# A mixture-of-experts decoder trunk on one Trainium2 core: where two engines leave the loop of an expert, how two norms are divided, and how two weight loads are cut

## The chip, the core and the metric

The kernel runs on one core of one Trainium2 chip. TensorE (PE in the profile) multiplies, VectorE (DVE), ScalarE (ACT) and GpSimd (POOL) work on elements, SyncE (SP) issues nearly all transfers, and 16 DMA engines move them. Each engine runs its own program; they meet at semaphores. The metric is the device time of the whole program in microseconds (us), median of the runs.

## What is computed

Two layers over 256 tokens of 1024 features, all in float32. Each layer: a mixer, cross-attention into 256 memory tokens, and a mixture of 32 experts of which each token takes 2. After each of the three, `x = LayerNorm(alpha * x + f(x))`. Cut to what matters here:

```
for layer in range(2):
    mix = even_mixer(x) if layer == 0 else (B * conv3(C * h)) @ w_out     # B, C, h = split(x @ od_w_in, 3)
    x = layer_norm(alpha * x + mix, ...)
    x = layer_norm(alpha * x + cross_attention(x, mem_k, mem_v), ...)
    x = layer_norm(alpha * x + moe(x), ...)        # moe: sum over the 2 experts of a token of
                                                   # gate * ((silu(x @ w1) * (x @ w3)) @ w2)
```

Each expert has three matrices of 2 MB (w1 and w3: 1024 x 512, w2: 512 x 1024). All 32 experts of both layers are read once: 192 matrices, about 400 MB of the 477 MB that the program moves.

## The kernel before

Tokens lie in two tiles of 128 (`TT = 2`). Twelve places in SBUF hold expert matrices: six of a ring, three named ones (SPARE, GAINS, HELD) and three slots (6, 7, 8) that serve the mixer and the attention in other stages. Four experts at a time have their three matrices in them (`SETS = 4`), and eight turns (`TURNS`) go over the 32 experts. GAINS also holds, in its first half (columns 0 to 2047), the gain and bias rows of the current norm (`gb`), and slot 8 holds the queries (first half) and the attention's output (second half).

**SP** issues the loads strictly in the order of its program, and each may wait for its place to come free. The first twelve are `first_load` (L435 on); the load of expert 2's w1 into GAINS stands last, behind the wait for both tiles of x (L457, L458). Then `next_expert` (L464) loads expert e + 4 when expert e has given its places back: w1 and w3 once the hidden product is done (`hid_done`), w2 once the result is (`y_done`). For the very last expert w3 and w2 are loaded in two transfers, 3072 columns (`MOST`) and then 1024, so that PE can begin before the rest has landed.

**PE** works by units of up to 32 tokens of one expert. An expert with more tokens has more units (m of them). A unit on PE is: `scatter` of the unit before (L1070), `turn` (L1051), `gather` of the next unit (L1028), `results` with w2 (L1062), and then `hidden` of the next unit with w1 and w3 (L1044). Before the hidden product of the last expert `keep_warm` issues `WARM = 18` products with zeros (L515).

**DVE** and **ACT** follow unit by unit. DVE: `build` the selection of the next unit (L1575), `silu_in`, `glu_out`, `turn` (L1589, L1594, L1599), `take` (L1585), `weight` (L1580). ACT: tanh (L1855), and the copies L1859 and L1861. Their loop over the units of an expert is a nest: 4 times `Fori` with an `If`, and in each 2 times an `If`, whatever m is. PE's loop leaves by a branch when m is reached.

**The norm behind the experts** starts from four PSUM banks that hold both tiles, q = 0 to 3 being four quarters of the features. DVE takes statistics (L1229), aggregates (L1168), POOL computes `rstd` (L1940, L1941), DVE the shift (L1237). ACT writes the normalized tile 0 (four operations, L1282) and half of tile 1, DVE the other half of tile 1 (L1252). PE transposes both tiles (L536), ACT (L1295) and DVE (L1174) write them into `xT`, and the mixer of layer 1 begins with `od_c0` by tile (L574) and goes on by weight (L566). In the last norm ACT writes both tiles, and DVE multiplies by the gain and adds the bias in four pairs of 512 columns (L1266, L1267); SP sends out four pieces in order (L496).

Of the kernel before, what the change touches and what calls it, by code (L numbers as in the profile page):

```python
# [58 lines left out]
WARM = 18  # L59
# [31 lines left out]
def program(nc, T, out):  # L91
    ctx = ExitStack()
    with ctx:
# [110 lines left out]
        rest_in = {m_: sem(f"rest_in_{('w1', 'w3', 'w2')[m_]}") for m_ in (1, 2)}  # L204
# [46 lines left out]
        dve_plain = sem("dve_plain")  # L251
        out_ready = sem("out_ready")
# [88 lines left out]
        def _(sp):  # L341
# [68 lines left out]
            for L in range(DEPTH):  # L410
# [24 lines left out]
                def first_load(e, m_):  # L435

                    s = slots[e][m_]
                    wait_free(s)
                    if e == SETS - 1 and m_:
                        sp.sem_inc(rest_in[m_], 16)  # L440
                    sp.dma_start(slot_ap(s), expert_weights(PARTS[m_], L, e)).then_inc(loaded[s], 16)

                for m_ in range(3):
                    first_load(0, m_)
                first_load(1, 0)
# [5 lines left out]
                first_load(2, 1)  # L451
                if L == 0:
                    sp.wait_ge(mem_kept, 16)
# [10 lines left out]
                def next_expert(e, j, last=False):  # L464

                    m, first = load_units(sp, L, e)
                    for m_ in range(3):
                        s = slots[j][m_]
                        sp.wait_ge(used_up[m_], first + m)
                        if m_ and last and j == SETS - 1:  # L470
                            src = expert_weights(PARTS[m_], L, e + SETS)
                            sp.dma_start(slot_ap(s)[:, 0:MOST], src[:, 0:MOST]).then_inc(loaded[s], 16)
                            sp.dma_start(slot_ap(s)[:, MOST:4096], src[:, MOST:4096]).then_inc(rest_in[m_], 16)
                            continue
                        if m_ and j == SETS - 1:
# [16 lines left out]
            for t in range(TT):  # L492
                for done, h in enumerate((1, 0)):
                    hh = slice(512 * h, 512 * (h + 1))
                    sp.wait_ge(out_ready, 2 * t + done + 1)
# [5 lines left out]
        def _(pe):  # L501
# [15 lines left out]
            def normal(i, t):  # L517

                if i % 3 == 2:
                    pe.wait_ge(act_plain[t], sum((Q, Q // 2)[t] for j in range(2, i + 1, 3)))  # L520
                    if t == 1:
                        pe.wait_ge(dve_plain, Q // 2 * (i // 3 + 1))
# [3 lines left out]
            def turned(key, src, t, warm=0, halves=(0, 1)):  # L526

                for h in halves:
                    ps = claim(pe, (key, t, h))
# [335 lines left out]
            for L in range(DEPTH):  # L865
                if L == 1:

                    for h in range(2):
                        wait_loaded(pe, f"od_c{h}")
                        pss = [claim(pe, ("odc", 4 * h + c)) for c in range(4)]  # L870
                        for c in range(4):
                            if h == 0 and c == 0:
                                for t in range(TT):
# [1113 lines left out]
```

## Time and profile before

| | us |
|---|---|
| median of 3 runs (lowest, highest) | 1385.27 (1383.77, 1385.79) |
| the profiled execution | 1383.4 |
| its span from first to last instruction | 1381.6 |
| PE busy | 1145.1 (83%) |
| DVE, ACT, POOL busy | 393.6, 168.8, 28.5 |
| mean granted TensorE clock | 0.929 |
| moved over the span | 477.40 MB, mean 346 GB/s |

The span is cut into 40 slices of 34.5 us in the page's second part. Two stretches stand out, about 310 to 712 us and 965 to 1365 us: the expert stages, in which DMA is 99% busy at 426 to 430 GB/s. Between and before them PE is at 9 tenths and the transfers pause at times.

### The profile page before, as it was taken

What the parts mean: (1) busy time and instruction counts of PE and PEld (TensorE: products, weight loads), DVE (VectorE), ACT (ScalarE), POOL (GpSimd) and SP (SyncE); (2) the same over time, 40 slices, a digit from 0 to 9 for tenths busy, and PEclk for the clock granted to TensorE, in tenths of its full rate; (3) what the DMA queues carried; (4) which work ended last, traced back from release to release, by engine and by line L of the source; (5) the groups of instructions that cost most, each with busy time, mean ns of one, the idle gap of its engine ahead of it and who ended that gap; (6) DMA issues with size and microseconds to landing.
All of it is one profiled execution on the core that took longest, in us unless ns stands there. A gap on an engine that the chain in (4) does not pass through costs nothing.

```text
span 1381.6 us, 33102 instructions
## 1 busy us (share of the span) xinstructions
PE 1145.1 (83%) x11896; PEld 731.1 (53%) x11897; DVE 393.6 (28%) x1030; ACT 168.8 (12%) x470; POOL 28.5 (2%) x83
## 2 busy tenths in 40 slices
PE   8999999987997677668699999999897767757756
PEld 7885558554553344335358867655454433434333
DVE  1972632342231221112132133253222111211213
ACT  1212502110110000001020001111110000000001
POOL 3000000000000000000000000000000000000000
PEclk9999999998998988889899999999999887888888
DMA  9756058499999999999996657465999999999996
GB/s 347 250 183 244 9 189 342 186 352 426 429 427 430 427 429 428 428 429 428 429 406 251 243 197 319 182 236 207 426 427 430 427 430 427 428 429 428 428 428 258
DMA packets 68378, 477.40 MB, mean 346 GB/s; under 512 B 8364, under 2 KB 13772, under 8 KB 43500
## 3 DMA queue, kind: packets, MB, share of 16 engines
q1 hardware_dynamic: 66284, 470.27, 83.0%
q0 software_dynamic: 2048, 6.47, 1.4%
q8 instruction: 34, 0.56, 0.2%
q14 instruction: 12, 0.10, 0.0%
HBM read 473.58 MB, written 3.15 MB: 345 GB/s over the span
## 4 chain that ended last, share of the span: by engine, by line
PE 56%; DMA 31%; SPq 5%; issue 4%; DVE 2%; another core or an unknown queue 1%; ACT 1%; ACTq 1%; POOL 0%; DVEq 0%
DMA slot<-in_moe_w_dram 20%; PE bank L566 12%; PE bank L1044 12%; DMA ring<-in_moe_w_dram 10%; PE bank L589 8%; SPq L477 5%; PE bank L1062 4%; PE bank L1070 3%; PE bank L1028 2%; PE bank L574 2%; PE bank L775 2%; PE bank L929 1%; PE bank L947 1%; PE bank L623 1%; PE bank L515 1%
## 5 line engine op out<-in xcount | busy, mean ns | idle before, releaser
L1044 PE MATMUL bank<-ring,xT 128*32 128x256 f32 x1920 | 177.7, 452 | 43.3 <-DMA ring<-in_moe_w_dram 43.3
L1044 PE MATMUL bank<-slot,xT 128*32 128x256 f32 x1120 | 163.7, 457 | 2.2 <-issue 2.2
L566 PE MATMUL bank<-xT,ring 128*128 128x256 f32 x656 | 143.3, 379 | 0.7 <-PE bank L566 0.7
L1044 PE MATMUL bank<-held,xT 128*32 128x256 f32 x608 | 89.1, 458 | 56.6 <-DMA slot<-in_moe_w_dram 46.4
L1044 PEld LDWEIGHTS bank<-ring,xT 128*32 128x32 f32 x1920 | 91.3, 129 | 84.1 <-issue 64.5
L566 PEld LDWEIGHTS bank<-xT,ring 128*128 128x128 f32 x656 | 124.1, 190 | 17.7 <-issue 1.1
L1589 DVE SCALAR_TENSOR_TENSOR xT<-xT,bank 64x256 f32<-64x256 f32 x73 | 30.3, 415 | 348.7 <-ACT xT L1855 348.6
L1044 PE MATMUL bank<-spare,xT 128*32 128x256 f32 x512 | 78.7, 475 | 45.6 <-DMA ring<-in_moe_w_dram 43.2
L589 PE MATMUL bank<-ring,slot 128*128 128x512 f32 x256 | 111.4, 593 | 0.8 <-PE bank L566 0.8
L1062 PE MATMUL bank<-ring,xT 128*32 128x256 f32 x1824 | 109.6, 381 | 1.9 <-DVE xT L1599 1.5
L1044 PE MATMUL bank<-gains,xT 128*32 128x256 f32 x512 | 74.5, 455 | 36.1 <-DMA slot<-in_moe_w_dram 36.1
L1070 PE MATMUL bank<-xT 32*128 32x256 f32 x1200 | 86.6, 400 | 21.2 <-issue 20.0
L1044 PEld LDWEIGHTS bank<-held,xT 128*32 128x32 f32 x608 | 48.2, 131 | 91.9 <-issue 78.7
L1575 DVE TENSOR_TENSOR xT<-iota,place 128x64 f32 (+1 forms) x73 | 16.4, 225 | 276.2 <-issue 273.6
L1855 ACT ACTIVATE xT<-bank 64x256 f32<-64x256 f32 x73 | 27.6, 377 | 516.3 <-PE bank L1044 494.3
L1070 PEld LDWEIGHTS bank<-xT 32*128 32x128 f32 x1200 | 55.1, 184 | 56.7 <-issue 53.5
L1044 PEld LDWEIGHTS bank<-spare,xT 128*32 128x32 f32 x512 | 42.0, 135 | 78.2 <-issue 68.4
L1062 PEld LDWEIGHTS bank<-ring,xT 128*32 128x32 f32 x1824 | 60.5, 110 | 42.4 <-issue 8.5
L1028 PE MATMUL bank<-x,xT 128*32 128x256 f32 x1200 | 81.2, 388 | 0.0
L589 PEld LDWEIGHTS bank<-ring,slot 128*128 128x128 f32 x256 | 48.2, 190 | 59.1 <-issue 59.0
L1044 PEld LDWEIGHTS bank<-slot,xT 128*32 128x32 f32 x1120 | 75.0, 131 | 3.2 <-issue 2.7
L1044 PEld LDWEIGHTS bank<-gains,xT 128*32 128x32 f32 x512 | 39.0, 130 | 66.3 <-issue 54.0
(290 smaller groups left out, 1110.1 us busy)
## 6 DMA issues: line engine op xcount, KB each, us to landing
ring<-in_moe_w_dram SPq DMA_DIRECT2D x94, 2048.0 KB, 46.4
slot<-in_moe_w_dram SPq DMA_DIRECT2D x46, 2048.0 KB, 48.3
held<-in_moe_w_dram SPq DMA_DIRECT2D x16, 2048.0 KB, 39.2
spare<-in_moe_w_dram SPq DMA_DIRECT2D x16, 2048.0 KB, 46.9
gains<-in_moe_w_dram SPq DMA_DIRECT2D x16, 2048.0 KB, 47.0
ring<-in_od_w_in_dram SPq DMA_DIRECT2D x6, 2048.0 KB, 21.2
ring<-in_xa_wq_dram SPq DMA_DIRECT2D x4, 2048.0 KB, 11.5
ring<-in_xa_wo_dram SPq DMA_DIRECT2D x4, 2048.0 KB, 12.5
```

The costliest lines, as they stand in the source:

```text
L477: sp.dma_start(slot_ap(s), expert_weights(PARTS[m_], L, e + SETS)).then_inc(loaded[s], 16)
L566: ins = mm(ps, w[:, k, c0:c0 + P], rhs[:, k, :], start=(k == 4), stop=(k == 3))
L574: ins = mm(ps[:, t * P:(t + 1) * P], w[:, k, c0:c0 + P], xT[:, k, t * P:(t + 1) * P], start=(k == 4), stop=(k == 3))
L589: ins = mm(ps[:, :], oT[:, k, t * P:(t + 1) * P], ws[h][:, k, :], start=(k == 0), stop=(k == KC - 1))
L775: ins = mm(ps[:, :], memT[:, k, t * P:(t + 1) * P], w[:, k, :], start=(k == 0), stop=(k == KC - 1))
L1028: ins = mm(bX[qs[q], 0:w], d[:, t, :], x[:, t, q * w:(q + 1) * w], start=(t == 0), stop=(t == TT - 1))
L1044: ins = mm(b1[qs[2 * m + h], 0:S], xg[:, k, :], ws[m][:, k, h, :, :], start=(k == 0), stop=(k == KC - 1))
L1062: ins = mm(bY[qs[q], 0:n], hidT[:, c, :], w[:, c, q * n:(q + 1) * n], start=(c == 0), stop=(c == 3))
L1070: ins = mm(acc[q][:, t * n:(t + 1) * n], cb[qs[q], t * P:(t + 1) * P], yy[qs[q], :], start=False, stop=final and t == TT - 1, skip_group_c ...
L1575: tt(disp, iota[:, at_].unsqueeze(1).to_broadcast([P, TT, CAP]), column(place, e).to_broadcast([P, TT, CAP]), ALU.is_equal).then_inc(fam.d ...
L1589: stt(out=glu, in0=th, scalar=1.0, in1=banks[5][0:P // 2, 0:S], op0=ALU.add, op1=ALU.mult).then_inc(fam.glu_done, 1)
L1855: act(th, banks[5][0:P // 2, 0:S], ACT.Tanh, scale=0.5).then_inc(fam.tanh_done, 1)
```

## The change

1. **Loops.** On DVE and ACT the nest over an expert's units becomes one `Fori` over up to 8 rounds with one branch out of it when the last unit is done, as PE has it.
2. **Early halves.** Half of the w1 of expert 2 (GAINS, columns 2048 to 4095) is loaded right behind expert 0's, once `wo_mix` is done, and half of the w2 of expert 3 (slot 8, columns 0 to 2047) once the attention is done with the queries. The other halves stay where the whole loads were. Both layers.
3. **The last expert.** w1 and w3 are both cut at 3072 columns, and the transfers go w1 and w3 up to 3072, then w1 and w3 from there, then w2 as before. `WARM` is 12 instead of 18.
4. **Norm of layer 0's experts.** Both tiles are divided alike: ACT writes quarters 2 and 3, DVE quarters 0 and 1. Tile 0 is written, transposed and put into xT before tile 1. The 4 warm products between the two tiles go.
5. **Mixer of layer 1.** PE does column group 0 of `od_c0` for tile 0, then transposes tile 1, then group 1 for tile 0, then groups 0 and 1 for tile 1, then 2 and 3 by weight. The banks of PSUM are given out accordingly.
6. **Last norm.** DVE computes (psum - mean) * gain for both tiles from PSUM (eight operations of 256 columns). For tile 0 ACT multiplies by rstd and POOL adds the bias; for tile 1 DVE does both in one operation per 512 columns.

```diff
-WARM = 18
+WARM = 12
@@ SP: first loads
+                early_load(2, 0, (weights_used, order.index(f"wo_mix{L}b") + 1), gains_early)
                 first_load(1, 0)
...
                 first_load(2, 1)
+                early_load(3, 2, (xa_done, L + 1), queries_early)
@@ SP: next_expert
+                    if last and j == SETS - 1:
+                        for parts in ((0, 1), (2,)):
+                            sp.wait_ge(used_up[parts[0]], first + m)
+                            for m_ in parts:
+                                s = slots[j][m_]
+                                src = expert_weights(PARTS[m_], L, e + SETS)
+                                sp.dma_start(slot_ap(s)[:, 0:MOST], src[:, 0:MOST]).then_inc(loaded[s], 16)
+                            for m_ in parts:
+                                s = slots[j][m_]
+                                src = expert_weights(PARTS[m_], L, e + SETS)
+                                sp.dma_start(slot_ap(s)[:, MOST:4096], src[:, MOST:4096]).then_inc(rest_in[m_], 16)
+                        return
@@ PE: mixer of layer 1
+                        if h == 0:
+                            pss = [claim(pe, ("odc", c), bank=6 + c) for c in range(2)]
+                            by_tile(2, "od_c0", 0, pss[0], 0)
+                            turned(("n", 2), x, 1, at=(4, 5))
+                            by_tile(2, "od_c0", P, pss[1], 0)
+                            for c in range(2):
+                                by_tile(2, "od_c0", c * P, pss[c], 1)
+                            pss += [claim(pe, ("odc", c), bank=c - 2) for c in range(2, 4)]
+                            rotation[0] = 4
@@ DVE: norm behind the experts
             stats(0, range(Q))
             moments(0)
             stats(1, MOE_ORDER[:2])
-            shifts(0)
+            if i < LAST_NORM:
+                shifts(0)
+                plain_part(0)
             stats(1, MOE_ORDER[2:])
             moments(1)
             if i < LAST_NORM:
+                to_xT(st, v, i, 0)
                 shifts(1)
+                plain_part(1)
...
             else:
...
+                        nc.vector.scalar_tensor_tensor(out=x[:, t, cols_], in0=ps[:, t * n:(t + 1) * n], scalar=mv[:, t, 0:1],
+                                                       in1=gb[:, 0, cols_], op0=ALU.subtract, op1=ALU.mult).then_inc(centred[t], 1)
...
+                    nc.vector.scalar_tensor_tensor(out=x[:, 1, hh], in0=x[:, 1, hh], scalar=rstd[:, 1, :], in1=gb[:, 1, hh],
+                                                   op0=ALU.mult, op1=ALU.add).then_inc(out_ready[1], 1)
@@ DVE: the loop of an expert
-                    with v.Fori(0, ROUNDS // 2) as ra:
-                        with v.If(m > ra * 2):
-                            with v.Fori(0, 2) as rb:
-                                with v.If(m > ra * 2 + rb):
+                    with v.Fori(0, ROUNDS) as r:
...
+                        v.br_lt(v.to_reg(m - r), 2, on_true=f"moe{L}_rows_next", on_false=f"moe{L}_rows_again")
@@ ACT: the last norm (the loop is changed as DVE's)
+                        act(x[:, 0, hh], x[:, 0, hh], ACT.Identity, scale=rstd[:, 0, :]).then_inc(scaled, 1)
@@ POOL: the last norm
+                    nc.gpsimd.tensor_tensor(x[:, t, hh], x[:, t, hh], gb[:, 1, hh], ALU.add).then_inc(out_ready[t], 1)
```

## Rows read from the trace of the kernel before

**Rows 1.** Windows: stretch, its us, busy by engine, granted clock, DMA share, GB/s

```profile
306.00:308.00 2.00, 2.00 (x45) 1.09 (x39) 0.00 (x0) 0.37 (x1) 0.00 (x0) 1.00 0.66 172
...
960.00:962.00 2.00, 2.00 (x44) 1.18 (x38) 0.00 (x0) 0.37 (x1) 0.00 (x0) 1.00 0.00 0
```

**Rows 2.** Timeline of SP: start, us, line, transfers issued, early in both expert stages

```profile
306.07 8.46 SPq L477 DMA_DIRECT2D ring<-in_moe_w_dram  x4
...
945.00 23.90 SPq L477 DMA_DIRECT2D ring<-in_moe_w_dram  x4
```

**Rows 3.** DMA issues between 306 and 307 us: size, us from issue to landing

```profile
ring<-in_moe_w_dram SPq DMA_DIRECT2D x1, 2048.0 KB, 8.4
```

**Rows 4.** Chain that ended last, in time: start, us, what, at both stages' begin

```profile
295.87 4.32 issue
...
951.32 1.93 PE bank L1062 x32
...
959.15 1.73 PE bank L1062 x32
```

**Rows 5.** Timelines of ACT and DVE in layer 1: [idle before it, until whom]

```profile
949.26 0.38 ACT L1855 ACTIVATE xT<-bank 64x256 f32<-64x256 f32 x1 [3.88 <-PE bank L1044]
...
952.62 0.23 DVE L1575 TENSOR_TENSOR xT<-iota,place 128x64 f32 x1 [0.62 <-DVE xT L1580]
...
972.11 0.23 DVE L1575 TENSOR_TENSOR xT<-iota,place 128x64 f32 x1 [4.52 <-issue]
```

**Rows 6.** Timeline, last expert of layer 1

```profile
1355.78 4.06 PE L515 MATMUL bank<-zero 128*128 128x512 bf16 x18
...
1364.78 0.19 POOL L1950 TENSOR_TENSOR vare<-vare,half 128x1 f32<-128x1 f32 x1 [447.64 <-DMA slot<-in_moe_w_dram]
...
1366.08 1.91 PE L1062 MATMUL bank<-slot,xT 128*32 128x256 f32 x32
```

**Rows 7.** Timeline of SP: the cut loads of w3, layer 1

```profile
1312.01 4.24 SPq L472 DMA_DIRECT2D ring<-in_moe_w_dram  x1
1316.29 4.24 SPq L473 DMA_DIRECT2D ring<-in_moe_w_dram  x1
```

**Rows 8.** DMA issues between 1300 and 1330 us: the same two, us to landing

```profile
ring<-in_moe_w_dram SPq DMA_DIRECT2D x1, 1536.0 KB, 47.7
...
ring<-in_moe_w_dram SPq DMA_DIRECT2D x1, 512.0 KB, 44.7
```

**Rows 9.** Timeline, norm behind layer 0's experts and begin of layer 1's mixer

```profile
720.76 1.93 ACT L1282 ACTIVATE x<-bank,shift,rstd 128x256 f32<-128x256 f32 x4 [4.14 <-DVE shift L1237]
721.43 0.26 DVE L1168 BATCH_NORM_AGGREGATE mv<-bn 128x2 f32<-128x24 f32 x1
...
722.74 1.17 PE L536 MATMUL bank<-ident,x 128*128 128x128 f32 x8 [1.80 <-ACT x L1282]
...
725.50 3.74 PE L574 MATMUL bank<-xT,ring 128*128 128x128 f32 x32
729.07 38.15 PE L566 MATMUL bank<-xT,ring 128*128 128x256 f32 x176
```

**Rows 10.** Timeline, last norm

```profile
1373.24 0.26 DVE L1168 BATCH_NORM_AGGREGATE mv<-bn 128x2 f32<-128x24 f32 x1
...
1373.89 0.92 POOL L1941 TENSOR_TENSOR rstd<-vare,half 128x1 f32<-128x1 f32 x1
...
1375.14 4.39 SPq L496 DMA_DIRECT2D out_dram<-x  x4
...
1378.47 0.69 DVE L1267 TENSOR_TENSOR x<-x,gains 128x512 f32<-128x512 f32 x1
```

**Rows 11.** Groups of POOL by form: count, busy us, mean ns, idle before

```profile
L1941 POOL TENSOR_TENSOR rstd<-vare,half 128x1 f32<-128x1 f32 x12 | 7.2, 599 | 1.0
...
L1890 POOL TENSOR_SCALAR residual<-ident 128x128 f32<-128x128 f32 x1 | 0.6, 564 | 0.1
```

**Rows 12.** Timeline of DVE in layer 0's convolution: 19 operations with a pointer scalar

```profile
52.63 7.60 DVE L1352 SCALAR_TENSOR_TENSOR slot<-slot,e 128x256 f32<-128x256 f32 x19
```

More of the change, by code:

```diff
@@ L250, in program @@
         act_plain = [sem(f"act_plain{t}") for t in range(TT)]
-        dve_plain = sem("dve_plain")
-        out_ready = sem("out_ready")
+        dve_plain = [sem(f"dve_plain{t}") for t in range(TT)]
+        out_ready = [sem(f"out_ready{t}") for t in range(TT)]
+        scaled = sem("scaled")
+        centred = [sem(f"centred{t}") for t in range(TT)]
         x_ready = [sem(f"x_ready{t}") for t in range(TT)]
@@ L469, in next_expert @@
                         sp.wait_ge(used_up[m_], first + m)
[L470 to L475, printed above, removed]
+                        if j == SETS - 1:
                             sp.sem_inc(rest_in[m_], 16)
@@ L1040, in hidden @@
                         if rest is not None and k * S * 2 == MOST:
+                            pe.wait_ge(rest_in[0], rest)
                             pe.wait_ge(rest_in[1], rest)
@@ L1113, in _ @@
                     start_sum(q, 1)
+                pe.wait_ge(gains_early, 16 * (L + 1))
+                pe.wait_ge(queries_early, 16 * (L + 1))
                 pe.wait_ge(units_ready, L + 1)
@@ L1275, in moe_norm_act @@
                 a.wait_ge(row_scale[t], L + 1)
-                for done, q in enumerate(MOE_ORDER):
-                    if t == 1 and i < LAST_NORM and q < 2:
-                        continue
+                for done, q in enumerate(MOE_ORDER[:2]):
                     ps = wait_filled(a, ("f", i, q))
@@ L1866, in _ @@
                     m, first = load_units(a, L, e)
-                    with a.Fori(0, ROUNDS // 2) as ra:
-                        with a.If(m > ra * 2):
-                            with a.Fori(0, 2) as rb:
-                                with a.If(m > ra * 2 + rb):
-                                    n = first + ra * 2 + rb + 1
-                                    first_half(fam, n)
-                                    second_half(fam, n, comb, y)
-                                a.nop()
+                    before = nc.cur_bb
+                    with a.Fori(0, ROUNDS) as r:
+                        n = first + r + 1
+                        first_half(fam, n)
+                        second_half(fam, n, comb, y)
+                        a.br_lt(a.to_reg(m - r), 2, on_true=f"moe{L}_tanh_next", on_false=f"moe{L}_tanh_again")
+                        nc.switch_bb(f"moe{L}_tanh_again")
                         a.nop()
-                moe_norm_act(a, 3 * L + 2)
+                    a.br(f"moe{L}_tanh_next")
+                    nc.switch_bb(f"moe{L}_tanh_next", parent=before)
                 if L + 1 < DEPTH:
-                    norm_act(a, 3 * L + 2)
+                    moe_norm_act(a, 3 * L + 2)
+                else:
+                    a.wait_ge(ln_rstd, 2 * LAST_NORM + 1)
+                    for done, h in enumerate((1, 0)):
+                        hh = slice(512 * h, 512 * (h + 1))
+                        a.wait_ge(centred[0], 2 * (done + 1))
+                        act(x[:, 0, hh], x[:, 0, hh], ACT.Identity, scale=rstd[:, 0, :]).then_inc(scaled, 1)
         @block.gpsimd
```

131 lines of the change are left out of this document (75 added, 56 removed).

## The prediction

> **What bounds the kernel now.** I read the page's second part first: it separates two stretches of saturated transfers from the stages ahead of them, in which PE is busy nearly all the time. So the program is a chain of five pieces: PE up to the first expert, a stream of weights, a compute tail with a norm and the second layer's mixer and attention, a second stream, and a last tail. A microsecond saved counts only if it lies in a piece's chain. Next I asked where each stream begins, since its length is fixed by bytes. In layer 0 the window 306 to 308 us has a DMA share of only 0.66 [rows 1]; SP issues at 306.07, when expert 0's result is done [rows 2], and that transfer lands after 8.4 us [rows 3]. One of 2 MB at 428 GB/s needs 4.9 us, so nothing was queued ahead of it: the stream starts there. In layer 1 the engines move nothing from 960 to 962 us [rows 1]. Four ring loads go out between 945.00 and 968.9 [rows 2]: the first is expert 0's w2, the next two expert 1's w1 and w3, at about 964.4, when its third hidden product ends. That is the start of the second stream. From there 81 matrices follow (96 less 12 preloaded and 3 sent earlier): 81 x 4.9 = 397 us, and 964.4 + 2 + 397 = 1363.4, which is where the saturated slices end. So both streams start when PE frees the places, and neither waits for the bytes before it.
>
> **Part 2, the early halves: nothing.** They take 1 MB each out of the queue ahead of the streams, 2.45 us apiece. But a stream that starts at a release finds the engines empty before the change too [rows 1, 3]; without the two halves they are idle somewhat longer. What they could cost: they go out in stages where later loads are for later experts, so a shift of 2.45 us meets no waiting PE, and their waits are the ones that the neighbouring load had anyway, so no queue is held. Bounds: 0 lost; gained at most what is idle in the windows 306 to 310 of layer 0, about 0.9 us (0.34 of 2 us [rows 1], and a little behind it), if PE's stall ahead of it shrank. I take 0.
>
> **Part 1, the loops.** DVE idles 4.52 us between the last work of one expert and the build for the next one when m is 1, and 0.62 us from one round to the next within an expert [rows 5]. How much of the 3.9 us between them is the nest's empty rounds, no row says; it is between 0 and 3.9, and I take the middle, 2, on DVE and ACT alike (each needs only 0.9 below). In the streams that is off the path, since PE itself waits for weights. In front of a stream it counts: at 949.26 ACT starts tanh 3.88 us after its last copy [rows 5], 0.9 us behind the end of the hidden product (it begins with the release at 945.00 and takes 3.4). PE has 2.5 us of scatter, turn and gather to cover it, and is late by the rest: a wait of 0.14 and a results product of 1.93 instead of 1.73 [rows 4], 0.34 us. Only one such change of expert (0 to 1) lies before the second stream's start, none before the first's. Gain 0.34 (0 to 0.5). Two places where loops end, ahead of both norms, have 4.14 us of slack on ACT [rows 9].
>
> The price of the branch out is not in this trace for DVE or ACT. PE has its form, and shows either nothing extra or a stall such as the 4.32 us "issue" at 295.87 [rows 4], the first time its loop runs. The Trainium skill (Runtime: NRT & Kernel Launch, Instruction fetch mechanics) says that a taken branch to code outside the two fetched pages waits for a fetch by DMA. By that rule the new exit could cost such a stall; whether it does depends on where the code falls. That is a rival below. I take 0 for it here.
>
> **Part 3, the last expert.** In both layers 18 warm products run from the end of results to the beginning of the last hidden product: 4.06 us from 1355.78 [rows 6], 0.2256 each, so six fewer are 1.35 us. They are on the path if the weights are there. Layer 1: the first part of w3 lands at 1312.01 + 47.7 = 1359.7, the rest at 1316.29 + 44.7 = 1361.0 [rows 7, 8]. With the old order, the hidden product would wait for 1359.7, and the six products would be worth 0.1 only. The new order takes 512 KB (1.2 us) of w1 out from in front: 1358.5, and warm ends at 1355.78 + 2.71 = 1358.5. The last two of eight steps come 2.6 us later, at 1361.1, against 1361.0 for the rest of w3, which is unchanged since the sum of the bytes is. Then w2: results start at 1366.08 - 1.35 = 1364.7, and POOL sees its first part at 1364.78 [rows 6]; the last quarter is wanted 1.4 us later and 512 KB behind. All four just fit. Gain 1.30, with 0.1 as the low end and 1.35 as the high one. In layer 0 the same things stand with more room (its warm ends 1.0 us later against its landings), so 1.35. PE is busy before and behind at a granted clock of 1.00, so fewer products lower nothing. Together 2.65.
>
> **Parts 4 and 5, the norm into the mixer.** Before: ACT's four operations end at 722.69 and PE transposes at 722.74; the tile products of column group 0 follow at 725.50 and 38.15 us for 11 groups by weight, 3.47 each, from 729.07 [rows 9]. So `od_c0` is done at 729.07 + 0.17 + 3 x 3.46 = 739.6 (0.17: the overlap of records). After: ACT writes two quarters by 720.76 + 1.93/2 = 721.7, DVE two of its own beside it, 0.40 each [rows 12]. Transposes 721.8 to 723.0. DVE's two push the last statistics and the aggregate from 721.43 to 722.2; rstd of tile 1 comes at most 1.6 us later (1373.24 to 1374.81 in the last norm [rows 10]); the four xT operations of tile 0, under 0.40 each, take 723.05 to 724.45, and only then come the shift and tile 1's quarters, 1.1 us, to 725.6. PE finishes group 0 of tile 0 at 724.75 and waits 0.9 us: transposes of tile 1 from 725.7 to 726.9, then three tile products of 3.58/2 = 1.79 to 732.2, then two by weight to 739.15. Gain 0.45. Ends: -0.5, if DVE's longer list puts tile 1 another 0.9 us back; +1.3, if PE's wait for tile 1 vanished. From here to the second stream PE is busy without a gap, so it counts in full.
>
> **Part 6, the last norm.** Everything in tile 1's statistics moves forward, because no shift is waited for: the aggregate at 1372.75 instead of 1373.24 [rows 10]. Then eight DVE operations of 256 columns from PSUM; one with a pointer scalar takes 7.60/19 = 0.40 [rows 12], so tile 0 is centred by 1373.8 (first half) and 1374.6, tile 1 by 1376.2, and its two final ones (0.69 each, as at 1378.47) end at 1377.6. ACT's multiplication of 512 columns is not in the trace; one of 256 takes 1.93/4 = 0.48 [rows 9], so it is between 0.48 and 0.96, and I take 0.8: 1374.6 and 1375.4. Then POOL, whose add of 128 x 512 is not in the trace either. Its only wide operation with arithmetic takes 564 ns for 128 columns [rows 11], its smallest some 190: 2.9 ns for a column, 1.6 us for 512. Two are 3.2 us, from 1374.6 to 1377.8. SP sends in order, tile 0 first: the third and fourth pieces, done at 1376.9 and 1377.6, queue behind POOL's, and the fourth goes at 1378.5, against about 1379.2 before (1375.14 + 4.39 less the issue itself) [rows 10]. Gain 0.65; POOL's L1941 took 0.92 at 1373.89, beside DVE's product of x and gains, against 0.599 in the mean [rows 10, 11], so I put 0.15 to that: 0.5. Ends: +1.5, if POOL keeps up and DVE is last; -1.2, if both adds are stretched as L1941 was (2.5 us each, the fourth piece at 1380.4).
>
> On this step the Trainium skill speaks against the change: GPSIMD Engine Reference (Engine selection; Key points) gives elementwise work to VectorE, says that GpSimd is about twice as slow for two inputs, and that it contends with a DVE instruction with two SBUF inputs. The row of L1941 agrees as to contention. An estimate from that page's 4497 ns for 2048 columns, by columns, is 1.1 us plus dispatch for one add; the sum would then be about 0.4 us better.
>
> **The sum.** 0 + 0.34 + 2.65 + 0.45 + 0.5 = 3.9 us off the profiled execution's 1383.4: 1379.5. That execution lies 1.9 below the median of the three, so I put the same difference there: 1385.27 - 3.9 = 1381.4.
>
> **The rivals.**
> *The streams are bound by their bytes.* Then the early halves would count: 2 MB in each layer, 4 x 2.45 = 9.8 us, and 1381.4 - 9.8 = 1371.6. Against it stand the idle windows just before both starts. For it, nothing in layer 1; in layer 0 the 0.9 us. Chance 0.04.
> *The landings take the warm products' place.* The four fits of part 3 have 0.1 us of room in layer 1. If a transfer more costs 0.5 us in each layer, or lands late, 2.65 becomes 1 to 1.5: 1382.8. Chance 0.13.
> *POOL becomes the end.* The low end of part 6: 1.7 worse, 1383.1. With the low end of parts 4 and 5 too, 1384. Chance 0.15.
> *Slower: code that has to be fetched.* PE has one stall of 4.32 us ahead of the first stream and none ahead of the second, in the same program text, so it hangs on where code and loads fall, and PE's code grows here. A stall of that size between 931 and 964 us, or from the new exits on DVE in that stretch, delays the second stream by 4.3, and in layer 0 gather and results ran 1.1 longer behind it at a lower clock: 5.4. It decides as soon as more than 3.9 of it lies before 964.4: 1381.4 + 5.4 = 1386.8, slower than before. Two such stalls: 1392. In the streams it costs nothing. Chance 0.12.
> *Better than the sum.* The layer 0 stall shrinks (0.9), POOL keeps up (1.0): 1379.5. Chance 0.11.
>
> **How the numbers follow.** The forecast has the remaining 0.45, with 1381.4. Its own bounds from the parts are about 1379.5 to 1383. Two in ten may be left out: the bytes rival and part of the slow one; so low 1378.3, high 1385.4. A measurement here tells apart about 0.2%, 2.8 us. Faster than 1382.5: most of the forecast (0.37 of 0.45), better (0.11), bytes (0.04), a third of the landings (0.05) and of POOL (0.05): 0.62. Slower than 1388.0: half of the slow rival, 0.07. Within: 0.31.
>
> **What would show it.** Two DMA windows of idle before the starts as now, and the transfer at about 306 us landing after 8.4 us again: the halves bring nothing. DVE's idle time before L1575 near 2.5 us instead of 4.5. L515 with 12 in 2.7 us in both layers, the last hidden product starting with no wait; a wait on DMA there is the second rival. PE idle about 0.9 us between the first tile products and the second transposes. The last out transfer released by POOL, with its adds at 1.6 us. An "issue" gap on PE or DVE of 2 us or more between the second stage's first unit and the stream's start is the slow rival; the prediction is wrong by as much as that gap.

## The result, and the profile after

The changed kernel takes 1376.03 us (median of 4 runs, 1375.57 to 1377.9) against 1384.66 for the kernel before beside it (1383.77 to 1385.79): ratio 0.9943, 95% interval 0.9930 to 0.9957. A second comparison, six runs on another occasion, gave 1377.52 against 1384.18: 0.9951 (0.9939 to 0.9963). So 6.7 to 8.6 us are gone by the medians, where 3.9 were forecast; both medians lie below the predicted range. One of the eleven executions of the kernel with GAINS's half alone took 4107.89 us and is not in its ratio.

The page of the changed kernel (span, busy time by engine, then the 40 slices):

```profile
span 1376.1 us, 30241 instructions
PE 1142.7 (83%) x11896; PEld 735.4 (53%) x11897; DVE 393.5 (29%) x1032; ACT 165.3 (12%) x462; POOL 30.5 (2%) x85
PEclk9999999998998898888999999999998888888888
DMA  9856059579999999999997657555999999999996
```

The shape is as before, with two saturated stretches. The difference has to be looked for piece by piece, so I cut the span at five events that both kernels have, and took a second profile of each kernel to see how far one profile can be trusted. The second profile of before is an execution of 1384.28 us. All values are us from one event to the next, each read off the start of a row in the timeline; the end is the page's span, which is given to 0.1 us:

| stretch | before | before, second | after | after, second | mean difference | forecast |
|---|---|---|---|---|---|---|
| start to first hidden product, layer 0 | 290.72 | 290.78 | 291.37 | 290.08 | 0.0 | 0 |
| to the warm products, layer 0 | 413.28 | 414.21 | 411.08 | 410.85 | -2.8 | 0 |
| to the first statistics (last expert) | 13.83 | 13.83 | 12.54 | 12.52 | -1.3 | -1.35 |
| to first hidden product, layer 1 (norm, mixer, attention) | 210.16 | 210.06 | 209.11 | 209.17 | -1.0 | -0.45 |
| to the warm products, layer 1 | 427.79 | 427.83 | 427.61 | 427.97 | 0.0 | -0.34 |
| to the first statistics (last expert) | 13.87 | 13.86 | 13.06 | 12.52 | -1.1 | -1.30 |
| to the end (last norm) | 11.95 | 11.94 | 11.33 | 11.29 | -0.6 | -0.5 |

The differences make 6.8 us. What the forecast lacked, 2.8 us net, is the size of the gain in the stretch for which it had nothing: the stream of layer 0 with what leads up to it. The misses of the other stretches are smaller and cancel. The zero of the first row is a mean of 291.37 and 290.08, so a single profile says little there.

What happens there, in the chain of waits of the changed kernel (start, us, what the chain ran through):

```profile
291.37 3.66 PE bank L1073 x64
295.04 1.49 PE bank L1026 x6
296.53 2.03 issue
298.55 1.15 PE bank L1099 x16
```

The "issue" gap behind expert 0 is 2.03 us; it was 4.32 [rows 4]. In this profile PE's clock, too, stayed up (not in every one with so short a gap, as shown further down). The windows (PE, PEld, DVE, ACT and POOL busy, then granted clock, DMA share, GB/s), first of after, then of before:

```profile
300.00:302.00 2.00, 2.00 (x41) 1.23 (x44) 0.76 (x2) 0.37 (x1) 0.00 (x0) 1.00 1.08 451
302.00:304.00 2.00, 2.00 (x40) 1.20 (x36) 0.23 (x1) 0.37 (x1) 0.00 (x0) 1.00 0.96 410
306.00:308.00 2.00, 1.71 (x26) 0.94 (x18) 1.04 (x4) 0.38 (x1) 0.00 (x0) 1.00 1.02 430
```

```profile
300.00:302.00 2.00, 1.81 (x22) 1.13 (x26) 1.48 (x5) 0.00 (x0) 0.00 (x0) 0.80 1.01 426
302.00:304.00 2.00, 2.00 (x20) 0.88 (x24) 0.10 (x1) 0.37 (x1) 0.00 (x0) 0.50 1.01 426
```

Before, the clock fell to 0.50 (1.2 GHz) behind the gap of 4.32 us and PE did 20 products in 2 us; after, it kept 1.00 (2.4 GHz) and did 40. And SP sends the transfer that opens the stream 11.5 us after the first hidden product, where it was 15.4: at 302.86 (SP's row, then the DMA answer for that issue: KB, us to landing).

```profile
302.86 8.48 SPq L500 DMA_DIRECT2D ring<-in_moe_w_dram  x4
ring<-in_moe_w_dram SPq DMA_DIRECT2D x1, 2048.0 KB, 10.7
```

It lands after 10.7 us, not 8.4 [rows 3]: now something is queued ahead of it, and the window 306 to 308 has a share of 1.02 where it had 0.66 [rows 1]. The stream of layer 0 no longer starts from empty engines.

How much that is worth can be read from the bytes. The rows below are the first 17 us behind the first hidden product and the rest up to the warm products, of before and then of after:

```profile
290.72:307.72 17.00, 12.68 (x172) 7.50 (x176) 3.88 (x14) 1.12 (x3) 0.00 (x0) 0.90 0.93 364
307.72:704.00 396.28, 306.71 (x4521) 175.29 (x4511) 84.26 (x245) 38.99 (x104) 0.00 (x0) 0.89 1.01 428
```

```profile
291.37:308.37 17.00, 14.68 (x222) 9.30 (x226) 5.50 (x19) 1.62 (x5) 0.00 (x0) 1.00 0.82 330
308.37:702.45 394.08, 302.97 (x4468) 176.66 (x4461) 82.31 (x240) 38.40 (x103) 0.00 (x0) 0.89 1.01 428
```

The rest runs at 428 GB/s in both, so its length is its bytes. In the first 17 us before moved 6.2 MB and after 5.6. But half of GAINS, 1.0 MB, had gone out long before in after. With the release where it was, after would have moved 5.2 MB here and gained nothing, as the engines would only have idled longer. So by this estimate the earlier release let 0.4 MB more through, 1.0 us of the 2.8. The other 1.8 us are not traced. Part of them is that PE reached the warm products with some 0.5 MB less moved in all, and that amount differs by 0.4 MB among the six profiles with the whole load in its old place.

### The profile page after: what moved, and what is told of

It is laid out like the page before. It is cut to its first block, busy times and chain, and to the rows that moved or that the text cites. A ratio compares the mean times of both kernels' runs of the same rounds, so it can differ in the third digit from the quotient of the medians.

```text
span 1376.1 us, 30241 instructions
## 1 busy us (share of the span) xinstructions
PE 1142.7 (83%) x11896; PEld 735.4 (53%) x11897; DVE 393.5 (29%) x1032; ACT 165.3 (12%) x462; POOL 30.5 (2%) x85
## 3 DMA queue, kind: packets, MB, share of 16 engines
q0 software_dynamic: 2048, 6.47, 1.4%
## 4 chain that ended last, share of the span: by engine, by line
PE 58%; DMA 31%; SPq 6%; issue 3%; another core or an unknown queue 1%; DVE 1%; ACT 0%; POOL 0%; DVEq 0%
DMA ring<-in_moe_w_dram 21%; PE bank L1073 13%; PE bank L588 12%; DMA slot<-in_moe_w_dram 10%; PE bank L611 8%; SPq L500 5%; PE bank L1091 4%; PE bank L1099 3%; PE bank L1056 2%; PE bank L596 2%; PE bank L797 2%; PE bank L957 1%; PE bank L975 1%; PE bank L645 1%
## 5 line engine op out<-in xcount | busy, mean ns | idle before, releaser
L1073 PE MATMUL bank<-ring,xT 128*32 128x256 f32 x1920 | 174.5, 447 | 40.1 <-DMA ring<-in_moe_w_dram 40.1
L1073 PE MATMUL bank<-slot,xT 128*32 128x256 f32 x1120 | 167.4, 465 | 2.9 <-issue 2.9
L1073 PE MATMUL bank<-held,xT 128*32 128x256 f32 x608 | 93.8, 470 | 57.3 <-DMA slot<-in_moe_w_dram 48.6
L588 PE MATMUL bank<-xT,ring 128*128 128x256 f32 x640 | 139.9, 379 | 0.7 <-PE bank L588 0.7
L588 PEld LDWEIGHTS bank<-xT,ring 128*128 128x128 f32 x640 | 121.1, 190 | 17.3 <-issue 1.1
L1091 PE MATMUL bank<-ring,xT 128*32 128x256 f32 x1824 | 108.9, 379 | 0.0
L1073 PEld LDWEIGHTS bank<-held,xT 128*32 128x32 f32 x608 | 57.7, 134 | 89.1 <-issue 71.0
```

The costliest lines, as they stand in the source:

```text
L588: ins = mm(ps, w[:, k, c0:c0 + P], rhs[:, k, :], start=(k == 4), stop=(k == 3))
L1073: ins = mm(b1[qs[2 * m + h], 0:S], xg[:, k, :], ws[m][:, k, h, :, :], start=(k == 0), stop=(k == KC - 1))
L1091: ins = mm(bY[qs[q], 0:n], hidT[:, c, :], w[:, c, q * n:(q + 1) * n], start=(c == 0), stop=(c == 3))
```

## The experiments

### Which part brings it: loops, halves, both

**Before, with part 1 alone** (the branch out on DVE and ACT):

```
-                    with v.Fori(0, ROUNDS // 2) as ra:
-                        with v.If(m > ra * 2):
-                            with v.Fori(0, 2) as rb:
-                                with v.If(m > ra * 2 + rb):
+                    with v.Fori(0, ROUNDS) as r:
...
+                        v.br_lt(v.to_reg(m - r), 2, on_true=f"moe{L}_rows_next", on_false=f"moe{L}_rows_again")
```

> The kernel before with part 1 alone (branch out on DVE and ACT). Theory A (the shorter idle time of DVE and ACT shortens PE's stall behind expert 0 and so both streams' starts): 2 to 4 us faster, the gap at about 296 us is near 2 us. Theory B (the stall is PE's own and is shorter because less is being transferred, by the early halves): 0.3 us faster, the gap stays 4.3 us.

Measured: 1384.06, ratio 0.9997 (0.9987 to 1.0007). PE's gap stands as before (first row, PE's timeline, idle time in brackets; second row, DVE's), while DVE idles 2.02 us ahead of its build where the old nest took 4.5:

```profile
299.67 2.09 PE L1070 MATMUL bank<-xT 32*128 32x256 f32 x16 [4.78 <-issue]
295.80 0.23 DVE L1575 TENSOR_TENSOR xT<-iota,place 128x64 f32 x1 [2.02 <-issue]
```

So the loops do not make the gain, and they do not shorten the stall.

**Before, with part 2 alone** (both early halves):

```
+                EARLY = {GAINS: slice(2048, 4096), 8: slice(0, 2048)}
+                late = {GAINS: slice(0, 2048), 8: slice(2048, 4096)}
+                early_load(2, 0, (weights_used, order.index(f"wo_mix{L}b") + 1), gains_early)
...
+                early_load(3, 2, (xa_done, L + 1), queries_early)
```

> The kernel before with part 2 alone (early halves). Theory A: nothing, within 0.3 us, as the stream restarts from empty engines at about 308 us. Theory B: the gap at 296 us shrinks, up to 2 us faster. The bytes theory: 2.45 to 9.8 us faster.

Measured: 1382.14, ratio 0.9982 (0.9972 to 0.9992), by the ratio 2.5 us faster. The part that I had put at nothing brings most of what is missing. PE's timeline:

```profile
297.20 1.15 PE L1084 MATMUL bank<-xT 32*128 32x256 f32 x16 [1.96 <-issue]
299.50 1.93 PE L1042 MATMUL bank<-x,xT 128*32 128x256 f32 x16 [0.79 <-DVE xT L1591]
```

The stall is 1.96 us, as in after. The second row is new: with the old nest DVE is late with the build, PE waits a second time, and behind it the clock falls to 0.50 here.

**Before, with both parts:**

```
(the two edits above together)
```

> Parts 1 and 2 together. If they are independent, the sum of the two runs beside it. If the loops make the first stream start so early that its bytes bind (expert 0's result done before the queue has run empty), the halves are worth 1 to 2.5 us more here than alone: 4 to 6 us faster than the kernel before in all, with no DMA idle window left between 297 and 310 us.

Measured: 1381.8, ratio 0.9979 (0.9970 to 0.9988), 0.3 us better than the halves alone, within the error. The 4 to 6 us of my second theory did not come. PE's stall is 2.48 us here, with no second wait, and the clock is 0.50 behind it all the same:

```profile
298.00:300.00 2.00, 2.00 (x17) 1.20 (x18) 0.00 (x0) 0.00 (x0) 0.00 (x0) 0.50 1.01 426
```

**The changed kernel again**, the same source:

```
(no edit)
```

> The changed kernel once more. Its four executions lie between 1375.57 and 1377.9, and the profiled one is the slowest. Theory A, the gain over the forecast is real and sits in front of the first stream: a second profile shows the same gap behind expert 0 (about 2 us instead of 4.3) and its result done 7 to 8 us after its hidden product, and the ratio is 0.993 to 0.996. Theory B, the difference to the forecast is the spread of single executions: the ratio comes nearer to 0.997.

It is the second comparison and the fourth column of the table.

### Why the halves shorten PE's stall

PE waits for nothing that the profile names. But the DMA records hold a queue of kind "instruction", and in each profile it moved exactly one packet of 16 KB between the first hidden product and PE's return. Each of these rows is the queue's line in a window of 0.1 us, of before from 295.7, and of after from 293.9 (packets, MB, share):

```profile
q8 instruction: 1, 0.02, 57.0%
```

```profile
q8 instruction: 1, 0.02, 60.5%
```

Put beside PE's return, for the kernels in which the load of expert 2's w1 (GAINS) differs:

| kernel | GAINS bytes sent shortly before expert 0's products | packet, us after the first hidden product | PE's return after the packet | stall |
|---|---|---|---|---|
| before | 2 MB | 5.0 | 4.5 | 4.32 |
| before, second | 2 MB | 5.4 | 4.4 | 4.70 |
| before + loops | 2 MB | 5.5 | 4.4 | 4.78 |
| before + slot 8's half | 2 MB | 4.8 | 4.5 | 4.13 |
| before + GAINS's half | 1 MB here, 1 MB long before | 2.7 | 4.5 | 2.02 |
| before + both halves | the same | 2.6 | 4.5 | 1.96 |
| before, GAINS held back | none | 2.6 | 4.9 | 2.30 |
| after | 1 MB here, 1 MB long before | 2.6 | 4.6 | 2.03 |

The other six profiles fit in: 5.4 and 5.8 us from the hidden product to the packet with 2 MB (the runs with 12 warm products and with the norm and mixer, stalls of 4.64 and 5.10), 2.6 to 3.1 us with 1 MB (stalls of 1.92 to 2.48). My reading: PE asks for its next code some time after the hidden product begins, and this packet goes through the same DMA engines behind what is queued there. 1 MB takes 2.45 us at 428 GB/s, and the packet moves by 2.4 to 2.9. With no GAINS bytes at all it comes no earlier than with 1 MB, so by then the queue no longer sets its time. The Trainium skill (Runtime: NRT & Kernel Launch, Instruction fetch mechanics) says that a taken branch outside the fetched pages waits for a fetch by DMA; the packet and the gap agree with that. The time from packet to return is 4.4 to 4.9 us in all fourteen. What the records don't show is which engine the packet belongs to, when it was asked for, and what fills the 3.5 us from its end to PE's return. Nor does every such packet come with a stall: before has two more, at 301.9 and 306.5 us, while PE is at work. Three runs were chosen to break this reading.

**GAINS's half alone:**

```
+                EARLY = {GAINS: slice(2048, 4096), 8: slice(0, 2048)}
+                late = {GAINS: slice(0, 2048)}
+                early_load(2, 0, (weights_used, order.index(f"wo_mix{L}b") + 1), gains_early)
```

> The kernel before with only the early half of expert 2's w1 (GAINS). Fetch theory: PE's stall behind expert 0 in layer 0 ends 4.5 to 4.6 us after the one packet of the instruction queue (295.7 before), and that packet waits on its DMA engine behind the late load into GAINS. With 1 MB instead of 2 MB there the packet comes 2.5 us sooner against the first hidden product (2.5 instead of 5.0 us behind its start), the stall is 2.0 us, and the time is that of both halves: 1.5 to 2.5 us faster than before. Bytes theory: half of what both halves gave, about 1.1 us, whatever the packet does.

Measured: 1381.97, ratio 0.9983 (0.9973 to 0.9993). The whole effect of part 2. PE's timeline:

```profile
297.35 1.15 PE L1083 MATMUL bank<-xT 32*128 32x256 f32 x16 [2.02 <-issue]
299.58 1.07 PE L1041 MATMUL bank<-x,xT 128*32 128x256 f32 x16 [0.72 <-DVE xT L1589]
```

```profile
302.00:304.00 2.00, 2.00 (x44) 1.43 (x37) 0.00 (x0) 0.37 (x1) 0.00 (x0) 1.00 1.02 434
```

This row is the window behind it, with the clock at 1.00 behind two waits of nearly the same length as those that lowered it with both halves. (A third wait of 0.53 us lies at its beginning.) So the lower clock is no fixed follower of the second wait.

**Slot 8's half alone:**

```
+                EARLY = {GAINS: slice(2048, 4096), 8: slice(0, 2048)}
+                late = {8: slice(2048, 4096)}
+                early_load(3, 2, (xa_done, L + 1), queries_early)
```

> The kernel before with only the early half of expert 3's w2 (slot 8). Fetch theory: the load into GAINS is issued at about 288 us in any case and flows for its own 5 us after its start, so the packet stays at 5.0 us behind the start of the first hidden product, the stall at 4.3 to 4.8, and the time is that of the kernel before, within 0.5 us. Bytes theory: about 1.1 us faster.

Measured: 1383.67, ratio 0.9999 (0.9990 to 1.0008). As many bytes are out of the way, and nothing is gained. The engines are merely less busy at 286 to 288 us, ahead of the GAINS load, which goes out at 288.56 with its 2 MB as ever:

```profile
286.00:288.00 2.00, 2.00 (x13) 1.79 (x12) 1.83 (x8) 0.00 (x0) 0.00 (x0) 1.00 0.60 254
300.27 2.09 PE L1083 MATMUL bank<-xT 32*128 32x256 f32 x16 [4.13 <-issue]
```

(The share in the first row was 0.95 before.) So it is the place of the bytes that counts and not their number. This run also answers a rival: like the run with GAINS's half it adds one wait to PE's program ahead of the loop, which moves PE's code as much, and the stall stays.

**The whole GAINS load held back** until expert 0's first hidden product is done, no half early:

```
+                sp.wait_ge(fam.hid_done, 1)
                 first_load(2, 0)
```

> The kernel before, with the whole load into GAINS held back until expert 0's hidden product is done, in both layers; nothing is loaded early. Fetch theory: no transfer stands in front of the packet, so it comes at most 2.5 us behind the start of the hidden product and the stall is 2.0 us or less; but 2 MB more follow in the stream, which begins at about 297 us, so that the whole is 0 to 3 us slower than the kernel before. If the stall is a matter of DVE's or ACT's loop or of PE's own program, it stays at 4.3 us or more.

Measured: 1385.88, ratio 1.0017 (1.0008 to 1.0026). SP's and PE's timelines:

```profile
293.69 0.33 SPq L441 DMA_DIRECT2D gains<-in_moe_w_dram  x1
297.37 1.15 PE L1071 MATMUL bank<-xT 32*128 32x256 f32 x16 [2.30 <-issue]
```

This is the cleanest test, since no byte is moved early, PE's program is that of before, and the queue is merely empty: the stall shrinks to 2.30 us all the same (I had put it at 2.0 or less). Yet the kernel is 2.3 us slower by the ratio, because the 2 MB (4.9 us) now fall into the stream, which by then is bound by bytes: 416.65 us from the first hidden product to the warm products against 413.7 before. A short stall is worth having only if the bytes that made room for it go out in idle time, and `wo_mix`'s end is such a time.

One more thing separates the two kinds, though not the cause, since the seven with the short stall are also the seven whose half of GAINS went out early. The stretch from the first hidden product to the warm products of layer 0 is 413.3 to 415.4 us in the six profiles with a stall over 4 us, and 410.9 to 412.8 in the seven with one of 1.9 to 2.5 us (GAINS held back aside).

### The loops, taken out of the changed kernel

```
-                    with v.Fori(0, ROUNDS) as r:
+                    with v.Fori(0, ROUNDS // 2) as ra:
+                        with v.If(m > ra * 2):
+                            with v.Fori(0, 2) as rb:
+                                with v.If(m > ra * 2 + rb):
```

> The changed kernel with the old nest of loops on DVE and ACT. With part 1 alone on the kernel before nothing was measured (0.9997). If it is worth nothing anywhere: the ratio of the changed kernel, 0.9943 to 0.9951. If it counts once the early halves are there (DVE's build for expert 1 comes at about 299 us instead of 297, PE waits 0.8 us a second time, its granted clock drops to 0.5, expert 0's result is 2 us later and DMA idles 0.5 us before 308): 0.3 to 1 us slower than the changed kernel, and another 0.3 us in layer 1 at the change from expert 0 to 1.

Measured: 1378.93 (6 runs), ratio 0.9958 (0.9943 to 0.9973), against 0.9943 and 0.9951 with the loops. The intervals overlap, so a gain of the loops isn't shown. What they do in the trace is:

```profile
298.75 0.23 DVE L1620 TENSOR_TENSOR xT<-iota,place 128x64 f32 x1 [4.65 <-issue]
299.04 1.94 PE L1056 MATMUL bank<-x,xT 128*32 128x256 f32 x16 [0.82 <-DVE xT L1620]
```

With the nest DVE starts the build 4.65 us after its last work, PE waits 0.82 us for it, and the clock is 0.50 in the window from 300 to 302. The second wait is the nest's; the lower clock can't be put down to it. In after a gap of 2.03 us alone left the clock at 1.00, but the changed kernel with one addition less on POOL (below), which has the new loops, shows one gap of 1.92 us and the lower clock (PE's timeline, then a window):

```profile
297.78 1.96 PE L1099 MATMUL bank<-xT 32*128 32x256 f32 x16 [1.92 <-issue]
298.00:300.00 2.00, 2.00 (x18) 1.22 (x14) 0.46 (x2) 0.00 (x0) 0.00 (x0) 0.50 1.01 426
```

As long as PE's stall was over 4 us, DVE's lateness was hidden behind it.

### The last expert: are the landings in the way?

**Before with 12 warm products, the old order of transfers:**

```
-WARM = 18
+WARM = 12
```

> The kernel before with 12 warm products and the old order of the last loads. By the landings: the full 1.35 us in layer 0, where w3's first part lands at 705.9 and the warm products end at 706.7, but only 0.1 in layer 1, where it lands at 1359.7 against 1358.5: PE shows about 1.2 us of idle time behind the warm products there. Together 1.4 us faster. If landings do not bind: 2.7 us faster and no idle time.

Measured: 1382.79, ratio 0.9984 (0.9975 to 0.9994). PE's timeline in layer 1:

```profile
1359.73 2.76 PE L515 MATMUL bank<-zero 128*128 128x512 bf16 x12
1362.66 0.41 PE L1044 MATMUL bank<-spare,xT 128*32 128x256 f32 x2 [0.17 <-DMA ring<-in_moe_w_dram]
```

The wait for the weights is 0.17 us; I had worked out 1.2 for the old order. That looks as if the landings cost nothing, but the landing has not moved. SP's row for w3's first part, and the DMA answer for it (KB, us to landing):

```profile
1314.76 4.24 SPq L472 DMA_DIRECT2D ring<-in_moe_w_dram  x1
ring<-in_moe_w_dram SPq DMA_DIRECT2D x1, 1536.0 KB, 47.8
```

It lands at 1362.6, 431.8 us behind layer 1's first hidden product; in before it was 431.7 [rows 7, 8]. What moved is the warm products: they start 428.95 us behind that product instead of 427.8, because the hidden product of the expert ahead ran longer at a lower clock, and so the weights had 1.1 us more time. PE ran that product from 1349.17 on; a window within it:

```profile
1350.00:1352.00 2.00, 2.00 (x24) 1.13 (x20) 0.00 (x0) 0.00 (x0) 0.00 (x0) 0.50 0.98 418
```

The last hidden product starts 431.9 us behind the first in this profile and in before. From the first hidden product to the statistics layer 1 takes 441.66 us here, 441.66 and 441.69 in the two profiles of before, and 440.67 and 440.50 in those of after. So in layer 1 the six products brought nothing by themselves, as the landing time had said, and the new order of transfers is what lets 1.0 to 1.2 us through. In layer 0 the same wait is 0.26 us, and from the warm products to the statistics it takes 12.81 us against 13.83 before and 12.54 and 12.52 in after. This is one profile. The time, 2.2 us less by the ratio with 0.8 to 3.5 as the interval, can't tell the 1.4 us of the landings from the 2.7 without them.

### The norm and the mixer of layer 1 alone

```
+            if i < LAST_NORM:
+                plain_part(0)
+                to_xT(st, v, i, 0)
...
+                            by_tile(2, "od_c0", 0, pss[0], 0)
+                            turned(("n", 2), x, 1, at=(4, 5))
```

> The kernel before with parts 4 and 5 alone (norm behind layer 0's experts by tile, mixer by tile; the last norm as before). Forecast from the trace of before: 0.45 us faster; the two profiles of the changed kernel show 1.0 us less from the first statistics to layer 1's first hidden product, of which some may belong to the loops. Here that stretch is 209.1 to 209.7 us instead of 210.1.

Measured: 1383.78, ratio 0.9991 (0.9981 to 1.0000), 1.2 us faster by the ratio and at the edge of the error. From the statistics of layer 0 to layer 1's first hidden product it takes 209.20 us, against 210.16 and 210.06 before. In after the same stretch begins so:

```profile
717.90 1.02 ACT L1321 ACTIVATE x<-bank,shift,rstd 128x256 f32<-128x256 f32 x2 [4.13 <-DVE shift L1267]
718.97 1.16 PE L558 MATMUL bank<-ident,x 128*128 128x128 f32 x8 [0.88 <-ACT x L1321]
720.73 2.02 PE L596 MATMUL bank<-xT,ring 128*128 128x128 f32 x16 [0.59 <-DVE xT L1204]
722.76 1.13 PE L558 MATMUL bank<-ident,x 128*128 128x128 f32 x8
723.72 5.52 PE L596 MATMUL bank<-xT,ring 128*128 128x128 f32 x48
```

ACT writes two quarters and not four [rows 9], PE follows 1.07 us behind its start, waits 0.59 us for DVE's xT, and then has tile 1 ready without a wait. I had put 0.9 us of idle time in front of the second transposes; there is none.

### The last norm with one addition on POOL

Tile 0's second half stays with ACT and POOL; its first half goes to DVE, as tile 1's do:

```
-                    for done, h in enumerate((1, 0)):
+                    for done, h in enumerate((1,)):
...
+                for t, h, done in ((0, 0, 1), (1, 1, 0), (1, 0, 1)):
```

> The changed kernel, but POOL adds the bias only to the first half of tile 0; the second half is done by DVE as tile 1 is (one operation with two SBUF inputs more), and ACT's second multiplication goes. In the changed kernel the first of DVE's two such operations takes 1.73 us and the second 0.74; POOL's two adds take 1.26 each. If the 1.0 us is DVE held by POOL's second add: all three of DVE's take 0.74 or less, the last one ends 0.3 us earlier, and the stretch from the first statistics to the end is 11.0 us instead of 11.3. If the long one is due to its place (the first after eight from PSUM): it stays at 1.7 us and the end is 0.7 us later.

Measured: 1377.17 (6 runs), ratio 0.9948 (0.9931 to 0.9964): not to be told from after. The rows of the lines concerned (duration min/median/max in ns), of after and then of this kernel:

```profile
L2014 POOL TENSOR_TENSOR x<-x,gains x2: 1256/1262/1267, 1369.7 to 1371.0; 128x512 f32<-128x512 f32 x2
L1309 DVE SCALAR_TENSOR_TENSOR x<-x,rstd,gains x2: 737/1232/1728, 1371.0 to 1372.7; 128x512 f32<-128x512 f32 x2
```

```profile
L1309 DVE SCALAR_TENSOR_TENSOR x<-x,rstd,gains x3: 741/743/743, 1371.0 to 1372.3; 128x512 f32<-128x512 f32 x3
```

POOL's two additions take the same 1.26 us each. It is DVE that pays: its first operation, begun while POOL's second addition runs, takes 1.73 us and not 0.74. Without that addition all three take 0.74, and the stretch from the statistics to the end is 10.86 us against 11.33 and 11.29. That is some 0.4 us less in one profile, too little to show in the times.

## Why the prediction was wrong, by its own steps

**Part 2, "the early halves: nothing": the step that failed.** Its premise was right, since the stream did begin at a release and from empty engines [rows 1 to 3]. What followed was wrong: I took the release as fixed, asked only what the halves save in bytes, and bounded the rest at 0.9 us "if PE's stall ahead of it shrank". That was a bound on the idle time of the engines and not on the stall, which was 4.32 us [rows 4] with a lower clock behind it. I had all rows to see it: the stall, its likely cause (the rival on code names it), a fetch that goes by DMA, and a GAINS load of 2 MB queued just there. I wrote that the stall hangs on where code and loads fall, and never asked what moving a load would do to it. Measured: the stall 2.3 to 2.8 us shorter, the stream's first transfer 4.0 us earlier in the mean of two profiles of each, the stretch 2.8 us shorter; part 2 alone 2.5 us faster (1.1 to 3.9), where I had 0. Of the stretch's 2.8 us the bytes account for 1.0, by the earlier release as worked out above; the place of the rest stays open. Part of the 4.0 us can't arrive, because the transfer is now queued on arrival and the release no longer sets the start: that is the first rival's mechanism, in layer 0 alone and for part of its price. That the packet is PE's code is the reading that fits all profiles, and not shown by name. Two smaller things lie between 1381.4 and 1376.03: the base, 1384.66 by four executions and not 1385.27, and the occasion, since the second comparison shows 6.7 us and not 8.6.

**Part 1: size right, place not.** DVE's idle time between experts fell from 4.5 us to between 1.8 and 2.0 (2.5 forecast). In layer 1 SP's release stands 40.2 us behind the first hidden product and not 40.5, the forecast 0.34; it does so with part 1 alone too, and is back at 40.6 when the loops are taken out of the changed kernel. But from there to the warm products nothing arrives: the stretch takes 427.6 and 428.0 against 427.8. In layer 0 I had said that no such change of expert lies before the stream's start. There is one, behind the long stall, and it is uncovered as soon as the stall shrinks (0.82 us of wait in the changed kernel with the old nest). Neither the run with part 1 alone nor the one without it settles its price.

**Part 3: right, its bound too.** 1.35 forecast and 1.3 measured in layer 0; in layer 1, 1.30 against 0.8 and 1.35, or 1.0 and 1.2 when the stretch ahead is counted in. The first of these profiles has a gap of 0.67 us for "issue" ahead of the scatter where the second has 0.28. The bound of 0.1 for the old order came out in the one profile that tests it: the last hidden product started when w3 landed, 431.9 us behind the first, as in before. The wait shown is only 0.17 us because PE arrived 1.1 us later.

**Parts 4 and 5: mechanism right, 1.0 for 0.45.** DVE finished tile 1 earlier than I had it, and the wait of 0.9 us that I subtracted didn't come; 0.59 came at another place. The value is inside the bounds (-0.5 to 1.3).

**Part 6: 0.65 for 0.5.** Within it two terms were off in opposite directions. POOL's addition takes 1.26 us, where I had drawn a line through operations of other widths to 1.6. The Trainium skill (GPSIMD Engine Reference, Elementwise — side-by-side cycle accounting) gives 4497 ns for an add of 2048 columns, by columns an estimate of 1.1 us plus dispatch; 1.26 is near it. And the contention that I feared for POOL fell on DVE, 1.0 us. The Trainium skill (SBUF — State Buffer, SBUF: two separate sides) says that of a DVE operation with two SBUF inputs and a GpSimd one that reads SBUF, whichever starts first keeps the ports and the other blocks. The rows agree: POOL's second addition began at about 1371.0, just before DVE's operation at 1371.05, and it was DVE's that was longer.

**The rivals.** Landings: no, with the new order of transfers. POOL as the end: no, DVE's last operation ends at 1373.4 and POOL's at 1372.2. A new stall for code on the slower side: no new gap of 2 us or more came with the branch out. "Better than the sum" named the right cause, the stall of layer 0, and priced it at 0.9 where that stretch brought 2.8. With those 1.9 us more the low end would have been 1376.4: the second comparison, 1377.52, lies above that, and the first, 1376.03, 0.4 below, less than the 1.5 between the two.

## What to carry to other kernels

Where an idle time that the profile calls "issue" ends a fixed time after a packet on the instruction queue, suspect a fetch of code, and test whether it moves with the data queued ahead of it: look at what is sent just before such a place, and send it earlier into idle time, not later into a stream. When a stall of several us lies ahead of a stream, ask what releases the stream's first transfer: here 4.0 us off that release were worth more than was counted in instructions, and yet not all arrived. Don't read a single wait in a profile as the cost of a landing before you have compared the times of the landing themselves. And when a stall shrinks, look on every other engine for what had been late by less.

## What was unexpected of the hardware

- The return of PE after the instruction packet took 4.4 to 4.9 us in all fourteen profiles, whatever was queued, and with nothing queued ahead of it 2.30 us of stall remained in sight.
- TensorE's granted clock fell to 0.50 (1.2 GHz) for some us, from within the gap or shortly behind it, in all six profiles in which the gap was over 4 us. In the eight with 1.9 to 2.5 us it went both ways, four times each. It fell behind 1.96 and 0.79, behind 1.92 and 0.82, behind 2.48 alone and behind 1.92 alone; it stayed at 1.00 (2.4 GHz) behind 2.03 and 1.94 alone, behind 2.02, 0.72 and 0.53, and behind 2.30, 0.45 and 0.53. What decides between them stays open.
- A DVE operation on two SBUF inputs took 1.73 us instead of 0.74 beside a POOL addition, which itself kept its 1.26; the eight DVE operations that read one input from PSUM kept their time beside the first addition (3.16 us for eight, 0.40 each, as [rows 12]).
- One profile isn't enough for half a microsecond: the same source gave 291.37 and 290.08 us up to the first hidden product, 413.28 and 414.21 us for the stream of layer 0, and 13.06 and 12.52 for the last expert of layer 1.
